# Attention rounds of a two-block network: the splitting of four weight tiles and the output parts take other places in a hand-written order

## The reference, cut to what matters

```python
h = h + 0.5 * swiglu(rmsnorm(h, norm_ffn1), ffn1_w1, ffn1_w3, ffn1_w2)      # stage ffn a
z = rmsnorm(h, norm_mix) @ w_in                                            # q, k, v, gates, u
o_nsa = nsa_attention(q, ...)     # 8 heads: compressed, selected and window attention, gated
o_s5  = s5_mixer(u, ...)          # diagonal state space scan, gelu, y * sigmoid(y @ w_glu + b)
h = h + concatenate([o_nsa, o_s5], axis=-1) @ w_out                        # the w_out tiles
h = h + 0.5 * swiglu(rmsnorm(h, norm_ffn2), ffn2_w1, ffn2_w3, ffn2_w2)      # stage ffn b
```

## Time and profile before

| | |
|---|---|
| median of 3 runs | 1995.72 us (1992.42 to 1997.05) |
| profiled execution, its own time | 1992.18 us |
| its span in the trace | 1990.4 us |
| mixing stage, attention rounds 0 to 33 | about 497 to 668 us of the span |
| PE busy | 1925.7 us, 97% of the span |
| VectorE (DVE) busy | 1188.6 us, 60% |
| ScalarE (ACT) busy | 818.6 us, 41% |
| POOL busy | 336.7 us, 17% |

### The profile page before, as it was taken

How to read it: one execution, slowest core, us unless ns; L and a number is a source line. 1 busy time by engine, 2 the same in 40 slices (tenths; PEclk the granted TensorE clock), 3 DMA queues, 4 the chain that set the end, 5 groups by cost and what they waited for, 6 DMA issues and landing times.

```text
span 1990.4 us, 22518 instructions
## 1 busy us (share of the span) xinstructions
PE 1925.7 (97%) x9010; PEld 1499.7 (75%) x9010; DVE 1188.6 (60%) x1519; ACT 818.6 (41%) x1211; POOL 336.7 (17%) x329
## 2 busy tenths in 40 slices
PE   7999999999898999999999899999999899999997
PEld 5888888777544778888888778876788778776786
DVE  5748444578864556656655787836753659447732
ACT  5322233311555343222334448545542466455521
POOL 2000000136320111001011211504201024114001
PEclk9999999999899999999999899999999899999998
DMA  6322323222101145555533222221233222221331
GB/s 218 104 78 92 116 89 102 97 66 98 43 1 64 64 162 179 203 165 192 183 112 100 80 93 85 85 97 42 74 96 95 85 82 85 85 85 32 96 95 43
DMA packets 53464, 197.27 MB, mean 99 GB/s; under 512 B 6000, under 2 KB 6512, under 8 KB 52848
## 3 DMA queue, kind: packets, MB, share of 16 engines
q1 hardware_dynamic: 43200, 160.55, 24.5%
q0 software_dynamic: 7648, 29.10, 4.5%
q10 hardware_dynamic: 2512, 6.18, 0.9%
HBM read 192.67 MB, written 2.10 MB: 98 GB/s over the span
## 4 chain that ended last, share of the span: by engine, by line
PE 83%; DVE 8%; ACT 3%; POOL 2%; issue 2%; DMA 1%; ACTq 0%; POOLq 0%; DVEq 0%; SPq 0%
PE PS L618 83%; DVE WLO L1682 1%; ACT WHI L1215 1%; DVE AR L1944 1%; DVE AR L2036 1%; DVE AR L1715 1%; DVE TMP L2285 1%; DVE H L2114 0%; PE PS L877 0%; DMA H<-in_xT 0%; ACT HX L1386 0%; POOL AR L2380 0%; DMA RAW<-in_w_out 0%; POOL ACC L2343 0%; ACT SQ L1230 0%
## 5 line engine op out<-in xcount | busy, mean ns | idle before, releaser
L618 PE MATMUL PS<-HNH,WHI 128*128 128x512 f32 x1632 | 657.7, 403 | 17.2 <-ACT HNH L1246 15.4
L1682 DVE TENSOR_TENSOR WLO<-RAW,WHI 128x1024 fp32r<-128x1024 f32 (+1 forms) x272 | 377.0, 1391 | 494.2 <-ACT WHI L1215 494.1
L618 PE MATMUL PS<-HNH,WLO 128*128 128x512 f32 x1632 | 639.2, 392 | 0.4 <-DVE WLO L1682 0.4
L1215 ACT ACTIVATE WHI<-RAW 128x1024 fp32r<-128x1024 f32 (+1 forms) x272 | 296.6, 1094 | 625.6 <-PE PS L618 572.2
L618 PE MATMUL PS<-HNL,WHI 128*128 128x512 f32 x1632 | 436.3, 390 | 0.1
L618 PEld LDWEIGHTS PS<-HNH,WHI 128*128 128x128 f32 x1632 | 308.2, 189 | 97.5 <-issue 21.9
L618 PEld LDWEIGHTS PS<-HNH,WLO 128*128 128x128 f32 x1632 | 308.6, 189 | 72.6 <-issue 9.1
L618 PEld LDWEIGHTS PS<-HNL,WHI 128*128 128x128 f32 x1632 | 307.4, 188 | 64.7 <-DVE HNL L1685 1.0
L2343 POOL TENSOR_TENSOR ACC<-ACC,SQ 128x512 f32<-128x512 f32 x46 | 62.3, 1354 | 802.8 <-ACT SQ L1230 801.8
L618 PE MATMUL PS<-AR 32*128 32x256 f32 (+14 forms) x852 | 162.8, 416 | 6.7 <-DVE AR L2007 2.1
L618 PE MATMUL PS<-HIDH,WLO 128*128 128x512 f32 x352 | 137.1, 390 | 1.3 <-DVE WLO L1682 1.3
(11 more groups left out here) (317 smaller groups left out, 2276.7 us busy)
## 6 DMA issues: line engine op xcount, KB each, us to landing
RAW<-in_w_in SPq DMA_DIRECT2D x80, 512.0 KB, 3.5
AR<-in_w_ada POOLq DMA_DIRECT2D x48, 512.0 KB, 4.0
RAW<-in_w13a SPq DMA_DIRECT2D x44, 512.0 KB, 3.4
RAW<-in_w13b SPq DMA_DIRECT2D x44, 512.0 KB, 3.6
RAW<-in_w_out SPq DMA_DIRECT2D x40, 512.0 KB, 3.5
RAW<-in_w2a SPq DMA_DIRECT2D x16, 704.0 KB, 4.0
RAW<-in_w2b SPq DMA_DIRECT2D x16, 704.0 KB, 5.3
RAW<-in_w_inA SPq DMA_DIRECT2D x12, 512.0 KB, 3.4
```

The source lines that it names most:

```text
L618: return pe.matmul(o, l, r, start=start, stop=stop, skip_group_check=True)
L1215: act.activation(hi_of(name, i), raw_of(name, i), ACT.Copy).then_inc(*HI.up(name, i))
L1682: dve.tensor_tensor(lo_of(name, i), raw_of(name, i), f32(hi_of(name, i)), S_).then_inc(*LO.up(name, i))
```

## The change

A new step `convert` stands near the end of rounds 2, 3, 21, 24, 25, 27, 28 and 30. It makes one call of `hi_next` on ACT and of `lo_next` on VectorE. The calls at `squeeze 1, c` and at `glu m` go. The number of calls is the same, eight, and so is what each converts:

| tile | before, in round | after, in round |
|---|---|---|
| w_out 0 | 2, at the head of squeeze 1, 2 | 21, after the scores |
| w_out 1 | 3, at the head of squeeze 1, 3 | 24, after the scores |
| w_out 2 | 26, at the head of glu 1 | 27, after glu 2 |
| w_out 3 | 28, at the head of glu 3 | 30, before s5_out 2 |

The four other calls convert nothing, before and after. `o_part 0..2` move from round 30 to 28, and `low 0..2` from round 31 to 29, ahead of `s5_out 0` and `1`. No instruction is added or removed, and no load is moved in the order of SP.

```diff
@@ mix_order @@
         if 24 < n < 29:
             yield "glu", n - 25
+        if n in (2, 3, 21, 24, 25, 27, 28, 30):
+            yield ("convert",)
+        if n == 28:
+            for i in range(3):
+                yield "o_part", i
+        if n == 29:
+            for i in range(3):
+                yield "low", i
         if n in (29, 30):
             yield "s5_out", 2 * n - 58
             yield "s5_out", 2 * n - 57
         if n in (30, 31):
             yield "low", 2 * n - 56
             yield "low", 2 * n - 55
-        if n == 30:
-            for i in range(3):
-                yield "o_part", i
-        if n == 31:
-            for i in range(3):
-                yield "low", i
@@ act_program @@
                 elif step == "squeeze":
                     z, c = at_
-                    hi_next()
+                    if z == 0:
+                        hi_next()
...
+                elif step == "convert":
+                    hi_next()
                 elif step == "glu":
-
                     m, = at_
-                    hi_next()
@@ dve_program @@
-                elif step == "squeeze":
+                elif step == "squeeze" and at_[0] == 0:
+                    lo_next()
+                elif step == "convert":
                     lo_next()
...
-                elif step == "glu":
-                    lo_next()
```

## The result

| | before | after |
|---|---|---|
| median of 4 runs, side by side | 1996.08 us (1992.42 to 1997.05) | 1983.69 us (1982.92 to 1984.78) |
| profiled execution, its own time | 1992.18 us | 1982.92 us |
| its span | 1990.4 us | 1981.2 us |

The ratio is 0.9942, 95% interval 0.9924 to 0.9959: faster by 12.4 us, where 6.3 were forecast. The changed kernel was timed ten more times; all 14 runs have a median of 1984.37 us. By these the change is worth about 9.2 us, and the two profiled executions differ by 9.26 us. The other 3 us of the 12.4 are the scatter of medians of four runs: 2.5 us of before, 0.7 of after.

The account below looks back on a forecast made before the run. TensorE, busy for 97% of the span, was taken as the bound. Gains of 6.0 + 0 + 0.3 = 6.3 us took the profiled 1992.2 to 1985.9; 3.5 added for a median gave 1989.4 us, range 1985.5 to 1993.5.

Parts of the forecast that it names:

- part 4: Round 30 and out_s5: a new wait lets 2.8 of 6.4 us arrive, and the low clock takes 2.5.
- the 3.5 us that were added for a median: Whole kernel: the profiled execution lay 3.5 us below the runs' median, 1995.7, so that was added to 1985.9.
- Part 1: Rounds 2 and 3: without the two conversions the S5 back step starts 6.0 us earlier; bounds 4.4 and 7 us.
- the 4.5 us by the rule of the Trainium skill: Early scans: VectorE and GpSimd block each other, so a second POOL step beside them leaves 4.5 us instead of 6.0.
- Part 2: Rounds 21 and 24: converting w_out 0 and 1 there costs 0, with 0.8 us left in round 24; bound 2.3 us.
- Part 3: Glu 1 and glu 3: w_out 2 leaving gains nothing, w_out 3 leaving ends the scores of round 30 6.4 us earlier.
- 2.8 arrive: Out_s5: `s5_out 2` and PE's last piece of w_out 0 come 2.8 us earlier, of 6.4 us gained.
- I price that at the same 2.5 us: Out_s5: the clock falls behind PE's new waits and costs 2.5 us, as behind the earlier 4.16 us wait.
- The clock holds at out_s5: Rival at out_s5: no low clock, so the late rounds give 2.8 us, 8.8 in all, 1986.9 us; chance 0.2.
- The partial case: Rival: POOL beside the early scans (-1.55 us) and 1.5 us more waiting at out_s5; gain 3.2, 1992.5 us; chance 0.17.
- no change: Rival: what the early rounds save is waited for later, as in the S5 steps; 1995.7 us; chance 0.07.
- slower: Rival in DVE's queue, rounds 24, 27 and 30: conversions make PE wait and halve the clock; 8.4 us slower, 2004.1; chance 0.06.

Follow-up runs that it names:

- crowded_24: Changed kernel with w_out 0 converted in round 24 too, instead of 21; one profiled execution, 1983.94 us.
- Before again: The kernel before, unedited, timed and profiled once more; 1993.91 us (11 runs), ratio 1.0004.
- outputs_only: Kernel before with only `o_part 0..2` moved to round 28 and `low 0..2` to round 29; 1993.64 us (11 runs), ratio 1.0000.
- parts_early: Changed kernel with w_out 3 converted at the end of round 31, all `s5_out` in round 29, `low 4..7` in 30, `low 0..2` in 31; 1977.72 us, again 1976.67.
- early_only: Kernel before with only the conversions of w_out 0 and 1 moved, to rounds 21 and 24; 1987.59 us (8 runs), ratio 0.9972.
- second_only: Kernel before with only the conversion of w_out 1 moved, from round 3 to 24; one profiled execution, 1992.53 us.
- last_behind: Changed kernel with w_out 3 converted at the end of round 31 instead of ahead of `s5_out 2`; 1980.39 us (6 runs), ratio 0.9933.
- late_old_outputs: Kernel before with only the conversions of w_out 2 and 3 moved, to rounds 27 and 30; 1991.68 us (11 runs), ratio 0.9990.

## Why the prediction was wrong

The direction and the mechanism held; the time is 1.8 us below the range, and the median of all 14 runs 1.1 us. Two terms failed: the price of the wait ahead of out_s5 (part 4, 1.5 us too dear), and the 3.5 us that were added for a median (2.1 us too many). By its steps, against the profiled executions:

**Part 1: right, and 0.4 us short.** The back step "starts at 514.6", 6.0 us earlier. Measured 514.60 against 520.61 before, and the chain held that distance: the next scans on DVE's timeline are 6.01 to 6.03 us earlier up to 539 us, and 6.46 from 553 us on; `glu 0` is 6.47 earlier. The 0.45 more came in the rounds in which PE waits about 2 us for L2079 and both kernels have a low clock of 1.7 us behind that (534 to 538 after, 540 to 546 before). DVE then waits for PE's scores, 1.70 us before (to 553.39) and 1.26 after (to 546.92), which is the difference. No second POOL step fell beside the scans: four took 2.40 us, before and after, so the 4.5 us by the rule of the Trainium skill (SBUF — State Buffer, "Who interferes with whom") were not called on. That a POOL step holds up the scans the trace does show: four scans take 1.61 us with POOL idle, 2.40 with one POOL step of 1.26 us beside them, and 3.95 in round 0, where POOL works 3.3 us beside them. In the group of 2.40 a single scan is 1.44 us long and the other three about 0.4 each. What a second step would have cost at this place no run shows.

**Part 2: right.** The exponentials of round 25 (bound by maxima at 602.03) did not hold the scores of round 26, which started at 604.72 without a wait; the cover was larger than the 0.8 us counted, as crowded_24 shows.

**Part 3: right.** `values` of round 30 were forecast for 630.8, which with the 6.47 us of part 1 is 624.3; they started at 624.21 with 0.17 us of idling. The scores were to follow 2.02 us later at full clock, at 626.35; they did at 626.24. Both conversions ran without a wait for a load.

**Part 4: mis-sized, twice.** This is the step of the working that failed: it let 2.8 us arrive and took 2.5 for the clock, and measured were 3.3 and 1.6. (a) "2.8 arrive": ACT's exponentials of round 30 were counted to 636.4, with two parts and the shares (0.6 us each) in front; less 6.47 that is 629.9, and they ended at 629.5, since the parts and the shares were done by 628.3. The conversion ended at 630.48, where the forecast has 637.45 less 6.47, 630.98. `s5_out 2` started at 631.65, 34.19 us behind `glu 0` against 37.53 before: 3.3 us. The piece of w_out 0 with part 7 moved by as much: (648.76 - 603.93) - (638.97 - 597.46) = 3.32. (b) "I price that at the same 2.5 us". From that piece to the flips of item 31 it is 654.67 - 648.76 = 5.91 before and 646.44 - 638.97 = 7.47 after: the low clock cost 1.56 us. Before, the wait of 4.16 us lost 3.4 us of clock; the three pieces of after, with 4.9 us in all, lost 1.7. So parts 3 and 4 gave 1.76 us, not 0.3. (The waits themselves were counted to about 6 us, and were 4.9.)

**What the sum did not hold.** 1.0 us came behind the flips of item 31, in code that the change does not touch. Up to 472 us behind them the PE waits stand at the same distances, to a tenth; 746 us behind them they are 1.1 us earlier after. In between two things happen. First after falls back by 0.6 us: around 1107 to 1125 us its low clock loses 8.5 us, where that of before (1118 to 1132) loses 6.8. Then before has a low clock that after has not, seen in its windows:

```profile
1302.00:1304.00 2.00, 2.00 (x6) 1.56 (x6) 0.00 (x0) 0.53 (x2) 0.00 (x0) 0.54 0.83 262
1304.00:1306.00 2.00, 2.00 (x7) 1.65 (x6) 0.00 (x0) 0.60 (x1) 0.00 (x0) 0.60 0.53 209
```

Before again, outputs_only and both profiles of parts_early have a low clock at this place of the program too; the other nine have none. PE did not idle ahead of it: it was busy for all 18 us from 1284 to 1302. What it did last was 32 matmuls of only 32 columns each, from 1298.26 on for 3.65 us. There are two such groups in the whole trace, and the low clock of parts_early at 1715 us comes in the second of them. So the place is the program's. What decides whether the clock falls there stays open: of the two executions of parts_early one fell at both and one at the first alone.

**The median.** The forecast added 3.5 us, the distance of the profiled execution to the median of three runs. Over all 60 runs beside the others (and over the 71) that distance is 1.4 us, and after has the same (1984.4 against 1982.9). This alone is 2.1 us of the miss. With 1.4 the forecast would have read 1987.3, which lies in the stated range, and with the measured sizes of part 4 (1.5 more), of part 1 (0.4) and of the stretch behind (1.0) 1984.4: measured 1984.4. The fit to a tenth is luck, as each term has a few tenths of its own. That the median of the first four runs of after was another 0.7 us lower than this is scatter.

**The rivals.** "The clock holds at out_s5" was wrong: it fell, and cost less than thought. Its total, 8.8 us, lies near the measured 9.2, but by the wrong step. Here the rule of the Trainium skill that the prediction set against the rows (TensorE: Matmul & The Clock Gate, "The HAM clock gate": the activity window runs freely, so the same wait may or may not be caught) agrees with the experiments: waits of 2.0 and 0.3 us at out_s5 left the clock at 1.00 in both profiles of before, and brought it to 0.50 in early_only, second_only and last_behind. The partial case is refuted by the scans (2.40 us) and the early stretch (6.4 us shorter after, 5.9 in early_only), those of no change and slower by the intervals; and the ground of the slower one by crowded_24. Of the signs that the prediction named, those of being right came: the rounds up to `glu 0` are 6.0 to 6.5 us earlier, PE waits for nothing of note in rounds 25 to 28, and there is a stall in out_s5 with a clock of 0.50 behind it.

## What to carry to other kernels

Put a conversion where both engines that do it idle, and read what stands behind it on the slower one: the same conversion cost 3.2 us at one place of the queue (w_out 3 ahead of `s5_out 2`, after against last_behind) and 0.5 at most at another (crowded_24). When a wait is moved to where the result is wanted, follow it to the end of that stretch and move what stands in front of it too: here that was worth another 7 us beside the 9 of the change. And ask three runs only for a direction: the base of a forecast is the median of many.

## What the runs showed of the hardware

The clock's loss came in equal pieces. In all fourteen profiles, the first 26 and the last 20 us of the span left out, each stretch of low clock lost 1.7 us, or two, three, four or five times that (3.4, 5.1, 6.8, 8.5), whatever wait stood before it. How much of a loss reaches the time depends on what PE does in it: late_old_outputs lost 3.4 us in the late stretch, after 1.7, and the stretches differ by 0.2 us. Behind the flips of item 31 before and after lost the same 13.7 us, and differ by 1.0. Over all fourteen, that stretch goes with its loss: 1333.5 us where 12.0 were lost (early_only), 1339.2 where it was 17.1 (parts_early), and 1334.7 to 1336.0 in the other twelve, with 13.7. The prediction took the price of a wait that had lost two pieces (3.4 us, of which 2.5 reached the time) for one that lost a single piece (1.6 reached it). A sum should take one piece for one wait, and say that it may be none or two: the waits of 2.0 and 0.3 us lost none or one, the wait of 2.4 us none, one or, in outputs_only, two.

Whether a given wait brings the clock down depends on more than its length. Kernels with equal waits at the same place differed in it, and executions of one kernel did in the stretch behind (parts_early, 1339.2 and 1335.5 us). It may also be what spreads single runs of before from 1990.8 to 1999.0 us, but those runs were not profiled.
